# Renewal one column later, sums spread over the columns, and another order of products at a feed-forward layer's start

## The reference

```python
def rmsnorm(x, g):
    return x * rsqrt(mean(x * x, axis=-1, keepdims=True) + EPS) * g
# first_block, after its attention
h2 = rms_norm(x, norm_ffn)
x = x + (silu(h2 @ w_ffn_gate) * (h2 @ w_ffn_up)) @ w_ffn_down
# second_block, for l in range(2)
x = x + 0.5 * swiglu(rmsnorm(x, ffn1_norm[l]), ffn1_w1[l], ffn1_w3[l], ffn1_w2[l])
...            # mixer, then cross attention
x = x + 0.5 * swiglu(rmsnorm(x, ffn2_norm[l]), ffn2_w1[l], ffn2_w3[l], ffn2_w2[l])
```

## Time and profile before

| | |
|---|---|
| median of 3 runs | 3253.48 us (3253.07 to 3253.67) |
| the profiled execution | 3252.73 us, its span 3250.8 us |
| PE busy | 3156.0 us (97%) |
| DVE busy | 2295.4 us (71%) |
| ACT busy | 1481.3 us (46%) |
| mean granted clock of TensorE | 0.99 of full |
| DMA | 314.60 MB, mean 97 GB/s |

### The profile page before, as it was taken

The page is one execution under the profiler, slowest core; times in us unless marked ns, Lnnn a source line. Parts: engine busy times, 40 slices in busy tenths (PEclk is TensorE's granted clock), DMA queues, the critical chain, the costliest instruction groups (busy, mean ns, idle before and its releaser), DMA issues. The chain is left out here.

```text
span 3250.8 us, 46287 instructions
## 1 busy us (share of the span) xinstructions
PE 3156.0 (97%) x18338; PEld 2747.0 (85%) x18338; DVE 2295.4 (71%) x3102; ACT 1481.3 (46%) x2317; POOL 0.2 (0%) x4
## 2 busy tenths in 40 slices
PE   9999999999999799999999899989999999989998
PEld 7777778779998699988887799969999888779998
DVE  6564455578886887866755877878886676478876
ACT  5663555544433543443533534444433454354433
POOL 0000000000000000000000000000000000000000
PEclk9999999999999899999999999999999999999999
DMA  4333333243332233222323233233332333133331
GB/s 145 102 94 98 101 94 110 85 136 97 104 100 94 74 104 104 85 88 79 122 86 104 78 98 104 78 104 95 102 104 65 101 97 110 47 123 103 99 104 53
DMA packets 90789, 314.60 MB, mean 97 GB/s; under 512 B 10192, under 2 KB 12624, under 8 KB 90192
## 3 DMA queue, kind: packets, MB, share of 16 engines
q1 hardware_dynamic: 83376, 294.69, 28.6%
q10 hardware_dynamic: 7200, 16.97, 1.8%
HBM read 309.52 MB, written 2.10 MB: 96 GB/s over the span
## 5 line engine op out<-in xcount | busy, mean ns | idle before, releaser
L2079 DVE TENSOR_TENSOR wlo<-raw,whi 128x1024 fp32r<-128x1024 f32 x353 | 428.6, 1223 | 248.6 <-ACT whi L1770 242.0
L1770 ACT ACTIVATE whi<-raw 128x1024 fp32r<-128x1024 f32 (+1 forms) x355 | 367.2, 1046 | 104.1 <-DMA raw<-in_weights 102.1
L1407 PE MATMUL ps<-x_hi,whi 128*128 128x512 f32 x800 | 333.1, 416 | 61.1 <-DVE x_lo L2155 41.1
L1407 PE MATMUL ps<-h_hi,whi 128*128 128x512 f32 (+1 forms) x845 | 328.8, 389 | 1.0 <-DVE x_back L2249 0.7
L1408 PE MATMUL ps<-h_lo,whi 128*128 128x512 f32 (+1 forms) x845 | 328.1, 388 | 0.0
L1409 PE MATMUL ps<-h_hi,wlo 128*128 128x512 f32 (+1 forms) x845 | 327.7, 388 | 0.0
L1409 PE MATMUL ps<-x_hi,wlo 128*128 128x512 f32 x800 | 317.5, 397 | 0.0
L1408 PE MATMUL ps<-x_lo,whi 128*128 128x512 f32 x800 | 317.1, 396 | 0.0
L2246 DVE SCALAR_TENSOR_TENSOR x_res<-ps,x_res 128x512 f32<-128x512 f32 (+1 forms) x253 | 173.9, 687 | 113.5 <-PE ps L1409 108.0
L1407 PEld LDWEIGHTS ps<-x_hi,whi 128*128 128x128 f32 x800 | 154.1, 193 | 106.0 <-DVE x_lo L2155 45.5
L2016 ACT ACTIVATE blocks<-blocks 128x512 f32<-128x512 f32 x110 | 69.6, 633 | 373.6 <-DVE blocks L2425 200.7
(11 more groups left out here) (355 smaller groups left out, 7952.0 us busy)
## 6 DMA issues: line engine op xcount, KB each, us to landing
raw<-in_weights SPq DMA_DIRECT2D x353, 512.0 KB, 3.5
form_A<-in_sets SPq DMA_DIRECT2D x200, 512.0 KB, 3.5
bias<-in_biasB ACTq DMA_DIRECT2D x16, 384.0 KB, 3.2
bias<-in_biasA ACTq DMA_DIRECT2D x16, 256.0 KB, 2.9
mem_raw<-in_mem ACTq DMA_DIRECT2D x3, 1024.0 KB, 5.1
x_res<-in_x SPq DMA_DIRECT2D x8, 256.0 KB, 6.2
x_res<-in_x ACTq DMA_DIRECT2D x8, 256.0 KB, 3.2
out_x<-x_res SPq DMA_DIRECT2D x16, 128.0 KB, 1.8
```

The source lines that it names most:

```text
L1407: pe.matmul(out, hi, xhi, start=start, stop=False)
L1770: return act.activation(out, in_, ACT.Copy, scale=scale)
L2079: dve.tensor_tensor(wlo[u % RING][:, :], raw[u % RING][:, :], whi[u % RING][:, :].bitcast(F32), ALU.subtract).then_inc(sems["unit_ready"], 1)
```

## The change

1. **Renewal a column later.** `renew` takes the place of `refresh` ahead of every feed-forward: ACT's half stays at its column, DVE's half (`resum`: `sq_sum` and `x_lo`) stands behind the next column's `evac`. The high half of a unit of weights is made behind a column and its low half behind the next (`raise_units`, `lower_units`).
2. **Sums in portions.** The moving sums' four parts stand one per column, each a column behind the part that it reads. The columns come as 0, 1, 2, 4, 5, 6, 3, 7 (`TAIL`), or, between two feed-forwards, as 0, 4, 1, 5, 2, 6, 3, 7 (`LINKED`), and the first `plain` takes its chunks in that order. The first pair's blocks are loaded one per column.
3. **Tail of a feed-forward.** The four columns over tiles 16 to 19 stay in PSUM banks 0 to 3 until their rest is added, so each has one `evac` in place of two. Before n = 2 and 6 the first pair's S1, S3, S2 and two low parts are formed in the last even pair of the layer ahead.
4. **Start.** The last moving sum, the roots and the forms stand in another order; units `u0+4` to `u0+7` are opened later (the even pair 2 and the first block of columns), and the forms of pair 3 move under that block. P1 and its `kept` stand ahead of the second hidden tile's rows.
5. **Odd pairs.** From pair 3 on, P4 of the pair ahead stands second, before P5.
6. The copy from `x_back` goes to ACT, with two buffers.

```diff
 HROWS = 5
+TAIL = (0, 1, 2, 4, 5, 6, 3, 7)
+SLOTS = ("S0", "S1", "T0", "T1")
+LINKED = (0, 4, 1, 5, 2, 6, 3, 7)
+AHEAD_SUMS = {1: 4, 2: 4, 5: 4, 6: 4, 9: 4}
...
+    def renew(m, n, j, gain, need=None):
+
+        late_refresh()
+        lower_units()
+        before_refresh(m, n)
+        step("refresh", n=n, m=m, gain=gain, need=need or ("evac", j), later=True)
+        late_sums.append(dict(s.steps[-1][1]))
+        if m == DC - 1:
...
+    def raise_units(upto):
+
+        while s.next_unit <= upto:
+            step("unit_high", u=s.next_unit)
+            raised.append(s.next_unit)
+            s.next_unit += 1
+
+    def lower_units():
+
+        while raised:
+            step("unit_low", u=raised.pop(0))
...
+    def before_refresh(m, n):
+
+        late_refresh()
+        t = moving.setdefault(n, dict(scaled=0, formed=0, high=0, low=0, rows=set()))
+        if m < DC - 1 and t["formed"] < t["scaled"]:
+            step("tform", n=n, p=t["formed"])
+            t["formed"] += 1
...
+        t["rows"].add(m)
+        if t["high"] < t["formed"]:
+            step("thigh", n=n, p=t["high"])
+            t["high"] += 1
+            t["fresh"] = True
+        raise_units(s.next_unit if upto is None else upto)
...
+        if t["low"] < t["high"] - t.pop("fresh", False):
+            step("tlow", n=n, p=t["low"])
+            t["low"] += 1
+        if t["scaled"] == t["formed"] < AHEAD_SUMS[n] and {t["scaled"], t["scaled"] + 4} <= t["rows"]:
+            step("xt", n=n, p=t["scaled"], gain=gain)
+            t["scaled"] += 1
...
-    for m in range(DC):
+    for m in TAIL:
         j = begun[m][1]() if m < 2 else column("w_out", 0, m, **merged(m))
-        step("refresh", n=norm, m=m, gain="norm_ffn", need=("evac", j))
-        toward_ffn(m, norm, "norm_ffn", j)
+        renew(m, norm, j, "norm_ffn")
+        after_refresh(m, norm, "norm_ffn", j, FIRST_SET)
...
-        s.open_units(u0 + AHEAD - 1)
-        step("ffn", n=n)
-        step("plain", n=n, unit=u0, c=0)
+        rest = moving_rest(n, gain)
+        early = not after_ffn
+        lower_units()
+        step("plain", n=n, unit=u0, c=0, rows=LINKED if after_ffn else TAIL)
...
-        high(1, "S2")
+        for go in rest[:-1]:
+            go()
+        raise_units(u0 + 3)
+        if early:
+            total(1, "S1")
+            high(1, "S1", "A11")
+            total(1, "S3", "S2")
         step("froot", n=n)
+        lower_units()
+        rest[-1]()
         step("fscale", n=n, unit=u0, c=0)
         row("silu", 0)
...
-        low(1, "S1")
+        if early:
+            step("wload", n=n, i=2, form="A22", free=("unit_free", u0 + 1))
+        if early:
+            high(1, "S2")
+            low(1, "S1")
...
-            product(i, "P1")
+            if o:
+                product(i, "P1")
...
+            if o:
+                kept(i, "P1")
+            if o:
+                s.open_units(u0 + 4 + 4 * (i // 2) + 3)
+            else:
+                high(i, "S4", "S3")
+                low(i, "S4", "S3")
+            if not o:
+                product(i, "P5")
+                kept(i, "P5")
             if o:
                 product(o, "P4")
...
-            if o:
+                product(i, "P5")
+                kept(i, "P5")
                 row("flow", 2 * o + 1)
...
-            more = q < PAIRS
+            more = q < PAIRS and i > 2 or i == PAIRS - 1 and linked
...
+            if i == 2:
+                s.open_units(u0 + 5)
...
-                if m == 0:
+                if b == 0 and m == 1:
+                    s.open_units(u0 + 7)
+                    high(q, "A11")
+                    total(q, "S1")
+                    high(q, "S1")
+                elif b == 0 and m == 2:
+                    total(q, "S3", "S2")
+                    high(q, "S2")
+                elif b == 0 and m == 3:
+                    low(q, "A11", "S1")
+                if m == (4 if b == 0 else 0):
                     total(q, "S4")
                     high(q, "S4")
...
+        step("ffn_end", n=n)
...
+        def parted(m):
+            return dict(rhs="h", n=T, evac="back" if back else "resid", m=m, c=c, rows=[row_slot(f) for f in fs], slot=SLOTS[m],
+                        need={row_slot(f): [("fhl", (n, f))] for f in fs} if m == 0 else {})
...
                 row("flow", NF - 1)
-            down(t1 + 4 * m, fs[0:4], m, fs[0:4] if m == 0 else ())
-        step("ffn_end", n=n)
-        for m in range(DC - last):
-            late = m < 4
-            j = down(t1 + (16 + 2 * m if late else 6 * m), fs[4:] if late else fs, m, fs[4:] if m == 0 else (),
-                     "back" if back else "resid")
-            step("refresh", n=n + 1, m=m, gain=gain_next, need=("x", m) if back else ("evac", j))
-            if back or gain_next.startswith("ffn1"):
-                toward_ffn(m, n + 1, gain_next, j)
+            partial[m] = first_rows(m)
+        for m in finish[:DC - last]:
+            j = last_rows(m) if m < 4 else down(t1 + finished[m], fs, m, (), "back" if back else "resid")
+            if linked:
+                renew(m, n + 1, j, gain_next, ("x", m) if back else None)
+                after_refresh(m, n + 1, gain_next, j, upto=(t1 + finished[m] + (1 if m < 4 else 5)) // UT + AHEAD + 1)
...
-        BACK = area("x_back", 100, [P, T])
+        BACK = [area("x_back_a", 100, [P, T]), area("x_back_b", 56, [P, T])]
...
+                elif kind == "evac" and a["evac"] == "back":
+                    m = a["m"]
+                    act.wait_ge(*on("evac", a["j"]))
+                    copy(X[:, m, :].rearrange("p (s r) -> p s r", r=NT),
+                         BACK[LINKED.index(m) % 2][:, :].rearrange("p (r s) -> p s r", r=NT))\
+                        .then_inc(*sig("x", m))
...
                     elif a["evac"] == "back":
-                        dve.tensor_tensor(BACK[:, :], out, X[:, m, :], ALU.add).then_inc(*sig("evac", a["j"]))
-                        after_own()
-
-                        dve.tensor_copy(X[:, m, :].rearrange("p (s r) -> p s r", r=NT),
-                                        BACK[:, :].rearrange("p (r s) -> p s r", r=NT)).then_inc(*sig("x", m))
+                        at = LINKED.index(m)
+                        if at > 1:
+                            dve.wait_ge(*on("x", LINKED[at - 2]))
+                        dve.tensor_tensor(BACK[at % 2][:, :], out, X[:, m, :], ALU.add).then_inc(*sig("evac", a["j"]))
                     else:
```

More of the change, by code:

```diff
@@ L520, in build_schedule @@
     norm = 1
[L522 to L537 removed]
+    moving = {}
@@ L614, in ffn @@
         total(1, "S4")
+        high(1, "A12")
         low(1, "S2")
         row("flow", 0)
-        high(1, "A12")
         low(1, "A12")
         step("fscale", n=n, unit=u0 + 2, c=2)
+        step("plain", n=n, unit=u0 + 3, c=3)
+        product(1, "P1")
+        kept(1, "P1")
         row("silu", 1)
-        step("plain", n=n, unit=u0 + 3, c=3)
         step("fscale", n=n, unit=u0 + 3, c=3)
@@ L987, in build_schedule @@
         norm += 1
[L988 removed]
+        for m in TAIL:
             j = begun[m][1]() if m < 3 else column("xa_wo_2", l, m, **attended(m))
[L990 to L991 removed]
+            renew(m, norm, j, f"ffn2_norm_2_{l}")
+            after_refresh(m, norm, f"ffn2_norm_2_{l}", j, FIRST_SET)
         last = l == LAYERS - 1
```

161 lines of the change are left out of this document (101 added, 60 removed).

## The result

The changed kernel takes 3180.91 us (median of four runs, 3180.04 to 3182.62) against 3253.43 (3253.07 to 3253.67): ratio 0.978, interval [0.976, 0.980]. Forecast were 3176 and a range of 3161 to 3202. 72.5 us were gained of 77.7 forecast. The profiled execution has a span of 3179.3 us, 71.5 less than before.

A forecast was written before the change was run, and what follows sets the result against it. PE, busy 97%, was taken to lose 96.4 us in waits and half clock at five feed-forward starts. Gains of 44.9 (n = 1, 5, 9) and 32.8 (n = 2, 6) make 77.7 us: forecast 3176 us, range 3161 to 3202.

The forecast's parts named there:

- What bounds it: Whole kernel: PE is busy 97%; its idle time and half clock, 96.4 us, lie almost all at five feed-forward starts.
- PE's need of 36.7 us: n = 1, 5, 9: PE's full-clock work from the last column to P7 of pair 1; 57.1 us at n = 2, 6.
- Renewal at n = 1, 5, 9: Columns there: DVE falls from 8.0 to 5.86 us per column without waits; PE's 5.5 us wait for `x_lo` shrinks to 0.7.
- The unit: Start of n = 1, 5, 9: `u0+3`, raised ahead of the root, no longer makes PE wait; the 2.19 us go.
- Both `kept`: Copies of P1 (1.5 us wait) and P6 (1.3 us): both waits go, with bounds 0 and 1.3 for P6.
- The linked starts: n = 2 and 6: DVE's work bounds; 6.3 us of waits and 2 of clock remain at each, 32.8 us go.
- the 2 us taken: n = 2 and 6: half-clock loss left at each start behind 6.3 us of waits, bounds 0 and 5.
- ACT's copy: Copy from `x_back` ahead of n = 2: 0.65 us each on ACT, upper end 1.05, which would add 3.2 us.
- Evacuations saved: Tail of a feed-forward: 20 x 0.69 us saved on DVE lie beside running products, so gain 0, also with banks held.
- odd pairs: New order of products in odd pairs: nothing gained, since PE never waits there; P4 and P3 have their inputs in time.
- DVE and ACT hold the linked starts: Rival at n = 2 and 6: the two engines take turns waiting, 17 us less gain, 3193 us; chance 0.15.
- The signs: Predicted traces: `x_lo` waits 10 to 15 us, all at n = 2, 6; windows 37 to 38 and 64 to 66.

The follow-up runs named there:

- experiment 2: Changed kernel, but ahead of n = 1, 5 and 9 columns in natural order, each renewed at once with whole moving sums, as before the change: 3205.14 us.
- experiment 1: Changed kernel, but every column renewed at once, ahead of the next one's evacuation, with sums still in portions: 3179.65 us.
- experiment 3: Changed kernel with unit `u0+3` put behind root and silu: first form 3180.59 us (nothing moved at n = 1, 5, 9), second, not raised with last column, 3191.52.
- experiment 8: Changed kernel, at n = 2 and 6 one sum ahead and `u0+3` early: 3175.23 us; also renewing at once at n = 1, 5, 9: 3172.77.
- experiment 4: Changed kernel with the `x_back` copy on DVE again: 3185.84 us; with it on ACT, walked the other way: 3182.59 in one run.
- experiments 5 and 6: Changed kernel with P5 second and P4 third in odd pairs again: 3180.34 us; with the first four last columns evacuated twice again: 3178.38.

## Why the prediction was right, point by point

**What bounds it: right.** Nearly all the gain came from the five starts: 73.3 us in the windows, against 71.5 in the whole span. Between the starts 1.8 us net were lost, and the wait for `x_k` alone is 1.9.

**PE's need of 36.7 us: 0.65 too small.** The windows at n = 1, 5 and 9 were to be 37.4; they are 38.2. Of that the wait is 0.69 (0.7 forecast) and the `kept` of P6 0.18 to 0.22. The rest is PE's own work, 37.3 to 37.35 us: from the last column to P1 it takes 22.8 without the wait (23.49 - 0.69), where I had 22.3 for four plain products and `fsum`, and from P1 to P7 14.55, where I had 14.4. Most of the 0.5 us is `fsum`: its two matmuls and the slower start behind them cost 0.87 us (702.39 to 703.49 in the timeline, less one pace of 0.23), where I had 0.5, and the first product behind the wait adds 0.1. So each start had 0.65 us less to give, 3.3 in five. This is the largest mis-sized term.

**Renewal at n = 1, 5, 9: size right, credit wrong.** Evacuation 0.92 behind (0.9 forecast), last `x_lo` 5.4 (5.5), rest 0.69, 0.70 and 0.71 (0.7). The part is worth 24.2 us (experiment 2). But the delay by a column, to which I gave the 0.77 us of each column, gives nothing; a low part standing between evacuation and sum of squares does the same, and better (experiment 1). The first part of the change was thus right in its size for a reason that does not hold: the waits inside the column go, but the delay is not what takes them away.

**The unit: right.** It follows the last `x_lo` and is worth 3.0 us at each of the three starts (experiment 3), somewhat more than the 2.19 read from the earlier trace rows, since PE now comes earlier. The cover of 3.5 us by `fscale` is about 4: it ends 19.3 us behind the last column (19.6 forecast), and P1 starts 23.5 behind (23.1).

```profile
714.74 0.68 DVE L2554 TENSOR_TENSOR blocks<-ps,rstd_x 128x512 f32<-128x512 f32 x1
...
719.62 0.28 PE L1836 MATMUL ps<-x_hi,form_hi_A 128*128 128x256 f32 x1
```

**Both `kept`: right.** That of P1 has gone, that of P6 left 0.2 of the 1.3 that I allowed.

**The linked starts: right in the mechanism, off in two parts that nearly cancel.** PE's waits at n = 2:

```profile
1046.57 0.50 PE L1544 MATMUL ps<-x_hi,whi 128*128 128x512 f32 x1 [1.60 <-DVE x_lo L2304]
...
1050.15 0.79 PE L1544 MATMUL ps<-x_hi,whi 128*128 128x512 f32 x1 [2.62 <-DVE x_lo L2304]
...
1053.21 0.79 PE L1544 MATMUL ps<-x_hi,whi 128*128 128x512 f32 x1 [1.41 <-DVE x_lo L2304]
```

5.6 us in three pieces (6.3 in two or three forecast), 5.2 at n = 6. The clock cost more than the 2 us taken: 66.7 - 57.75 (57.1 and the 0.65 above) - 5.6 = 3.3 at n = 2, and 65.97 - 57.75 - 5.2 = 3.0 at n = 6. These two are remainders. At n = 6 of experiment 8, where the clock stayed at 1.00, PE is busy 58.03 us and not 57.75, so up to 0.3 us of each may belong to PE's need instead. The 2 us were also low by their own proportion: 4.1 us for 10.6 of idle time and 8.5 for 19.3 give 2.4 to 2.8 for 6.3. The stretch in which the clock was down at n = 2 (windows view), in which PE's 6.44 us of work would have taken half as long at full clock:

```profile
1047.80:1058.00 10.20, 6.44 (x12) 3.98 (x13) 7.33 (x12) 7.72 (x11) 0.00 (x0) 0.50 0.19 53
```

So the two gave 30.9 us, where 32.8 were forecast.

**ACT's copy: the price was outside my bounds, the time almost untouched.** It takes 1.13 us at the median, above the 1.05 that I had as the upper end; 0.65 was the value taken. The 6% that I followed was misread. The earlier trace rows compare DVE's copy with an addition that reads PSUM. DVE's own copy in order of the same size stands in the trace of the kernel before:

```profile
L2148 DVE COPY sq_sum<-sq x14: 294/427/430, 16.9 to 3219.3; 128x512 f32<-128x512 f32 x11, 128x256 f32<-128x256 f32 x3
```

So the layout costs DVE 0.30 us (0.73 against 0.43), not 0.04, and ACT 0.50 (1.13 against 0.63; the row is the square, and the copy `h_hi<-blocks` of the same size takes 0.625). Nevertheless n = 2 waits only 0.4 us longer than n = 6, which has no such copy: DVE was the bound, as experiment 4 shows, with 8.0 us per two columns at both starts. ACT was close behind. At n = 2 DVE waited once for the square that stands behind the copy:

```profile
1051.80 0.69 DVE L2299 TENSOR_TENSOR sq_sum<-sq_sum,sq 128x512 f32<-128x512 f32 x1 [0.52 <-ACT sq L1971]
```

By the Trainium skill (SBUF — State Buffer, Door 1: The DMA port swizzle) an access that leaves a 16-byte line each time pays a penalty. Of the two readings weighed in the prediction the trace agrees with this rule, on ACT with 1.13 against 0.63 us and on DVE with 0.73 against 0.43; whether the lines are the reason on DVE no run separates.

**Evacuations saved, odd pairs: right that they bring nothing** (experiments 5 and 6). Behind the five starts no product of a pair waits, and DVE's 82% in the stretch shown is no bound. Wrong was to look for the price of the kept banks only beside them: it appeared in the cross attention.

**Sum.** 77.7 forecast, 71.5 found in the profiled spans: -3.3 for PE's need, -2.3 for the clock, -0.6 for the `kept` of P6, -1.9 for `x_k`, +1.8 for the shorter waits at n = 2 and 6. That is 71.4. Of the rivals none came about. Of "DVE and ACT hold the linked starts" there was the clock's part in the smaller size of 3, and DVE without slack (8.0 us per two columns, where the prediction had 7.4). Of the turns that it spoke of there was one wait, the 0.52 us above.

**The signs.** Most came as named: no wait for `wlo` L2079 is left, the two kinds of `kept` are at 0.6 us together, the clock is 1.00 at n = 1, 5, 9, the last evacuation is 0.92 behind and P1 does not wait. Four did not quite. `x_lo` is at 15.9 us, above 10 to 15, and not all of it is at n = 2 and 6: 10.9 are, 2.1 are the three rests that the sum had and the sign forgot, and 2.9 are two waits behind the feed-forwards n = 2 and 6, of 1.46 each, where the kernel before has 1.56 and 1.51. The windows of 38.2 and 66.7 lie just above 37 to 38 and 64 to 66. DVE has the wait of 0.52 inside a column at n = 2. And one product of a pair does wait, P7 of pair 1, 0.18 to 0.22 us at n = 1, 5 and 9; by the words of the prediction this was a sign of being wrong, by its sum it was within the bounds for the `kept` of P6.

## What to carry to other kernels

Ahead of a step that waits for another engine's answer put an instruction that is due anyway and as long as that answer takes; this does what a delay by a whole iteration does, without making the last iteration late. When a queue is relieved at a wait, list all that stands behind the next long step in it, since the next wait is there and not where the last one was. A change in the count of jobs shifts every rotation by modulus behind it: compare PE's waits in stages that the change does not touch.
